# 64-feature attention two heads at a time, with GpSimd scaling the exponentials

## The reference, cut to what matters

```python
# layer 0, 8 heads: softmax over a band of 128 tokens, with a sink ("ea", bias table evb)
s = einsum('qd,kd->qk', q, k) * 64**-0.5 + bias          # masked outside the band
p = exp(s - max(s)); p = p / (sum(p) + exp(sink - max))   # o = p @ v
# layer 0, 8 heads: stick breaking ("eb"), strictly causal
a = exp(log_sigmoid(z) + log_after)                       # log_after: reverse cumulative sum of log_sigmoid(-z)
# layer 1, 16 heads: causal softmax, three dilated patterns merged in one bias table per head ("oc", odb)
# sparse block, 16 heads: causal softmax over chosen keys, one mask for all heads ("sx", s_sel)
```

## Time and profile before

| | |
|---|---|
| median of 3 runs (3391.88 to 3395.95) | 3394.07 us |
| the profiled execution's own time | 3395.51 us |
| its span, first to last instruction | 3393.7 us |
| mean granted TensorE clock | 0.975 of full speed |
| PE busy | 3284.9 us, 97% of the span |
| DVE, ACT, POOL busy | 1454.8, 1157.3, 220.9 us |
| chain that ended last | PE 90%, DVE 5%, ACT 3%, POOL 1% |

### The profile page before, as it was taken

The page is one execution under the profiler, slowest core; times in us unless marked ns, Lnnn a source line. Parts: engine busy times, 40 slices in busy tenths (PEclk is TensorE's granted clock), DMA queues, the critical chain, the costliest instruction groups (busy, mean ns, idle before and its releaser), DMA issues.

```text
span 3393.7 us, 36847 instructions
## 1 busy us (share of the span) xinstructions
PE 3284.9 (97%) x14548; PEld 2627.4 (77%) x14548; DVE 1454.8 (43%) x2354; ACT 1157.3 (34%) x1887; POOL 220.9 (7%) x439
## 2 busy tenths in 40 slices
PE   8999998999999999999999999999999999989998
PEld 6888775777788888887866877888887785768887
DVE  3332337554333243323555543332325766543332
ACT  3232334343322133223344533332226624332221
POOL 1000100010000000000400100000132100010000
PEclk9999998999999999999999999999989999989999
DMA  4322220231332323332312412333222230223331
GB/s 140 100 94 99 87 81 1 87 124 50 93 100 94 99 89 96 96 100 87 99 59 66 138 50 86 95 93 100 73 87 75 73 109 5 75 71 97 100 100 68
DMA packets 212605, 291.44 MB, mean 86 GB/s; under 512 B 13872, under 2 KB 135984, under 8 KB 212304
## 3 DMA queue, kind: packets, MB, share of 16 engines
q1 hardware_dynamic: 209792, 279.59, 26.3%
q0 software_dynamic: 2640, 9.50, 0.9%
HBM read 286.94 MB, written 2.10 MB: 85 GB/s over the span
## 4 chain that ended last, share of the span: by engine, by line
PE 90%; DVE 5%; ACT 3%; POOL 1%; issue 1%; DMA 0%; POOLq 0%; DVEq 0%; ACTq 0%
PE ps L94 87%; PE ps L97 3%; DVE ebQ L115 1%; DVE hTl L109 0%; ACT xn L100 0%; POOL stat L103 0%; DVE ebP L103 0%; ACT L100 0%; DVE ebPT L121 0%; DVE s_ri L115 0%; POOL s_ri L103 0%; DVE xn L106 0%; ACT wh L100 0%; POOL e_ss L103 0%; ACT hTh L100 0%
## 5 line engine op out<-in xcount | busy, mean ns | idle before, releaser
L103 DVE TENSOR_TENSOR wl<-raw,wh 128x1024 fp32r<-128x1024 f32 (+1 forms) x530 | 640.9, 1216 | 1249.5 <-ACT wh L100 1244.4
L100 ACT ACTIVATE wh<-raw 128x1024 fp32r<-128x1024 f32 (+1 forms) x530 | 552.4, 1051 | 1362.0 <-PE ps L94 1318.2
L94 PE MATMUL ps<-hTh,wh 128*128 128x512 f32 x2144 | 841.1, 392 | 16.6 <-DVE hTl L109 16.6
L94 PE MATMUL ps<-hTl,wh 128*128 128x512 f32 x2144 | 838.1, 391 | 0.0
L94 PE MATMUL ps<-hTh,wl 128*128 128x512 f32 x2144 | 837.6, 391 | 0.0
L94 PEld LDWEIGHTS ps<-hTh,wh 128*128 128x128 f32 x2144 | 404.9, 189 | 104.4 <-DVE hTl L109 13.7
L94 PEld LDWEIGHTS ps<-hTl,wh 128*128 128x128 f32 x2144 | 405.1, 189 | 84.7 <-issue 1.0
L94 PEld LDWEIGHTS ps<-hTh,wl 128*128 128x128 f32 x2144 | 404.9, 189 | 84.8
L94 PE MATMUL ps<-wh,hTh 128*128 128x512 f32 (+2 forms) x832 | 324.2, 390 | 10.0 <-DVE hTl L109 5.8
L94 PE MATMUL ps<-wl,hTh 128*128 128x512 f32 (+2 forms) x832 | 321.4, 386 | 0.0
L94 PE MATMUL ps<-wh,hTl 128*128 128x512 f32 (+2 forms) x832 | 321.4, 386 | 0.0
(11 more groups left out here) (347 smaller groups left out, 4076.1 us busy)
## 6 DMA issues: line engine op xcount, KB each, us to landing
raw<-in_ffn_w_gu SPq DMA_DIRECT2D x352, 256.0 KB, 3.1
raw<-in_ffn_w_down SPq DMA_DIRECT2D x88, 512.0 KB, 3.5
raw<-in_xa_w_kv SPq DMA_DIRECT2D x32, 512.0 KB, 4.0
raw<-in_w_in SPq DMA_DIRECT2D x32, 512.0 KB, 3.7
raw<-in_od_w_in SPq DMA_DIRECT2D x24, 512.0 KB, 3.6
raw<-in_w_ffn_gate SPq DMA_DIRECT2D x44, 256.0 KB, 2.9
raw<-in_w_ffn_up SPq DMA_DIRECT2D x44, 256.0 KB, 3.1
raw<-in_w_ffn_down SPq DMA_DIRECT2D x22, 512.0 KB, 3.8
```

Source lines behind the costliest of these rows:

```text
L94: return self.made(lambda e: e.matmul(*a, **k))
L100: return self.made(lambda e: e.activation(*a, **k))
L103: return self.made(lambda e: e.tensor_tensor(*a, **k))
```

## The change

`Heads` becomes `Pairs` for the four 64-feature stages: a step s now handles heads 2s and 2s + 1 (u = 0, 1).

- PE issues the score products of the two heads in turn, block by block, and the value products likewise. The blocks go in the order 3, then 2 and 0, then 1 (in the band: 2 and 3, then 1 and 0). Four banks hold scores (two groups of a pair of heads), three banks turned rows, one bank the outputs.
- The blocks' scaling by the reciprocal moves from DVE to POOL (`pool_pairs`). One reciprocal (128x8) serves both heads. It stands on DVE behind `first` of the following pair.
- ACT copies all turned groups of the even head, DVE all those of the odd head. In the stick-breaking stage ACT copies both.
- The turned rows have one buffer for each head of the pair (before: two buffers, taken in turn by successive heads).
- POOL fills four `ebQ` buffers instead of two.
- In "oc" POOL issues the bias tables of pair s + 1 behind the scaling of pair s − 1.

```diff
-            self.sgroups = [[0, 1], [2], [3]] if self.causal else [[0, 1], [2, 3]]
-            self.groups = [[3], [2, 0], [1]] if self.causal else [[0, 1], [2, 3]]
-            self.tbank = 6 - len(self.groups)
+CAUSAL_GROUPS = [[3], [2, 0], [1]]
+BAND_GROUPS = [[2, 3], [1, 0]]
+        def sbank(self, s, n, u):
+            return 2 * ((s * len(self.groups) + n) % 2) + u
+        def tbank(self, s, u, n):
+            return 4 + ((2 * s + u) * len(self.groups) + n) % 3
...
+    def pe_pairs(pe, A, qT, kT, qkey, kkey, kv_of, V, vkeys):
+        def scores(s):
...
+                for both in zip(*parts):
+                    for u, (i, W, dst) in enumerate(both):
+                        k0, k1, _, _ = A.spans[i]
+                        r = slice(64 * u, 64 * u + 64)
+                        ins = pe.matmul(dst, qT[r, s, i * P:(i + 1) * P], kT[r, kb, k0 * P:k1 * P], start=True, stop=True)
...
+        def turn(s):
+            for u in range(2):
+                for n, group in enumerate(A.groups):
+                    b, at = A.tbank(s, u, n), 0
+                    pe.wait_ge(drained, pe.held[b])
+                    pe.held[b] = (A.tag, s, "t", n, u)
+                    for i in group:
+                        k0, k1, o, W = A.spans[i]
+                        pe.wait_ge(normed, (A.tag, s, u, i))
...
+            if A.total == CAUSAL_W:
+                for kt in range(NT):
+                    for u in range(2):
+                        ins = pe.matmul(o_[64 * u:64 * u + 64, kt * P:S], V(2 * s + u, kt), A.pt[u][:, kt, kt * P:S],
+                                        start=kt == 0, stop=kt == NT - 1)
...
+        for s in range(A.N + 2):
+            if s < A.N:
+                scores(s)
+            if s >= 2:
+                values(s - 2)
+            if 1 <= s <= A.N:
+                turn(s - 1)
+
+    def turned_out(e, A, s, u):
+        for n, group in enumerate(A.groups):
+            e.wait_ge(turned, (A.tag, s, n, u))
+            if s >= 1:
+                e.wait_ge(valued, (A.tag, s - 1))
+            put_turned(e, A.pt[u], bank[A.tbank(s, u, n)], A.spans, group, (A.tag, s, n, u)).also(
+                drained, (A.tag, s, "t", n, u))
+
+    def pool_pairs(pool, A, before=none):
+        for s in range(A.N):
+            before(s)
+            rd = A.small(s, 0, 4), A.small(s, 1, 4)
+            pool.wait_ge(step, (A.tag, s, "r"))
+            for u in range(2):
+                for group in A.groups:
+                    for i in group:
+                        pool.tensor_scalar(A.row(s, u, i), A.row(s, u, i), rd[u][:, i:i + 1], None, ALU.mult).then_inc(
+                            normed, (A.tag, s, u, i))
+
+    def act_pairs(act, A, O, base_, gone):
...
+        for s in range(A.N + 2):
+            if s < A.N:
+                (sigmoids if A.stick else exps)(s)
+            if s >= 2:
+                act.wait_ge(valued, (A.tag, s - 2))
+                act_hi(act, bank[VBANK][:, :], O, base_ + s - 2, slice(0, S), gone)
+            if 1 <= s <= A.N:
+                turned_out(act, A, s - 1, 0)
+                if A.stick:
+                    turned_out(act, A, s - 1, 1)
+
+    def dve_pairs(dve, A, O, base_, bias=None):
...
+        for s in range(A.N + 2):
+            if s < A.N:
+                (before if A.stick else first)(s)
+            if 1 <= s <= A.N:
+                (breaks if A.stick else later)(s - 1)
+            if s >= 2:
+                dve.wait_ge(valued, (A.tag, s - 2))
+                dve_lo(dve, bank[VBANK][:, :], O, base_ + s - 2, slice(0, S)).also(drained, (A.tag, "o", s - 2))
+            if 1 <= s <= A.N and not A.stick:
+                turned_out(dve, A, s - 1, 1)
...
     def pool_even(pool):
+        pool_pairs(pool, EA)
         handover(pool, "stick")
         pool.memset(EB.zr[:, :], 0.0).then_inc(step, "eb zero")
         for b in range(2):
-            pool.memset(EB.q[b][:, :], 1.0).then_inc(ones_set, "eb")
+            for u in range(2):
+                pool.memset(EB.q[b][u][:, :], 1.0).then_inc(ones_set, "eb")
```

More of the change, by code:

```diff
@@ L724, in scores @@
[L724 to L748, removed]
-            if s < A.H:
[L750 to L761, removed]
-            if 1 <= s <= A.H:
[L763 to L778, removed]
-                for n, group in enumerate(A.groups):
[L780 to L793, removed]
-                value(pe, h, A.pt[h % 2])
-        attend(pe, A, own)
@@ L838, in put_turned @@
             e.wait_ge(valued, (A.tag, h - 2))
-        for i in A.groups[n]:
-            k0, k1, o, W = A.spans[i]
-            src = bank[A.tbank + n][:, at:at + W].rearrange("p (k q) -> p k q", k=k1 - k0)
-            dst = A.pt[h % 2][:, k0:k1, i * P:(i + 1) * P]
-            if e.name == "act":
-                ins = e.activation(dst, src, AF.Copy)
-            else:
-                ins = e.tensor_copy(dst, src)
-            at += W
-        ins.then_inc(put, (A.tag, h, n)).also(drained, (A.tag, h, "t", n))
@@ new lines, in act_whole @@
+    def act_whole(act, A, finish):
+        for s in range(A.H + 3):
+            if s >= 3:
+                finish(s - 3)
+            if s < A.H:
+                nm, den = A.small(s, 1), A.small(s, 2)
+                act.wait_ge(maxed, (A.tag, s))
+                if s >= 2:
+                    act.wait_ge(turned, (A.tag, s - 2, 1))
+                for i in range(NT):
+                    ins = act.activation(A.row(s, i), A.score(s, i), AF.Exp, bias=nm[:, i:i + 1], scale=A.scale,
+                                         accum_out=den[:, i:i + 1])
+                    if i % 2:
+                        ins.then_inc(drained, (A.tag, s, "s", i // 2)).also(expd, (A.tag, s))
+            if 1 <= s <= A.H:
+                whole_turned(act, A, s - 1, 0)
@@ L1523, in pe_cross, with score @@
         A = C.A
-        def score(pe, h, i, dst, k0, k1):
+        def score(pe, h, i, dst):
             for c in range(2):
@@ L1544, in value @@
                 ins.then_inc(valued, (A.tag, h, c)).also(valued, (A.tag, h))
-        pe_attend(pe, A, score, value)
+        pe_whole(pe, A, score, value)
     def act_cross(act, C):
```

415 lines of the change are left out of this document (232 added, 183 removed).

## The result

The changed kernel takes 3446.61 us (median of 4 runs, 3442.7 to 3447.81) against 3392.98 (3391.11 to 3395.95) for the kernel before in the same comparison: a ratio of 1.0156, 95% interval 1.0144 to 1.0169. It is 53.6 us slower. The profiled execution took 3447.54 us, its span is 3445.8, its mean granted clock 0.956.

The account below looks back on a forecast made before the run. PE carried 90% of the chain; paired products would leave a nearly serial loop through ACT bounding oc and sx. Savings of 1.7 (oc), 2.7 (sx), 3 (eb) and 2.3 (ea), together 9.7 us, gave 3384.5 us, range 3366 to 3406.

Parts of the forecast that it names:

- the price of POOL's scaling: Scaling of one head's blocks on POOL: 1.8 us at its copy's price, at most 3.3 at its two-input operation's price.
- POOL is beside this loop: In oc and sx, POOL's scalings from F + 3.7 finish before needed: even head by F + 5.5, odd by F + 7.3.
- these 334 us: The four changed stages ea, eb, oc and sx, together 333.9 of the 3393.7 us span; the rest should cost the same.
- PE's work per pair: Two heads on PE at 2.4 GHz: scores 2.35, values 2.3, squares 2 × 1.24, about 7.1 us instead of 11.78.
- ACT's loop: In oc and sx, PE turns the odd head only after ACT's exponentials, `hTh` and first copy: 11.5 us a pair, high clock.
- F: The start of DVE's first reduction of pair s, from which the steps of the loop in oc and sx are timed.
- My middle of 12.5 a pair: Period assumed for oc and sx, between 11.5 us at the high clock and F + 13.5 after a clock fall.
- rival 2: Loop at the low clock throughout, with longer handovers: 13.5 us a pair plus 0.3, +10, 3404 us; chance 0.23.
- Rival 3: POOL at its two-input price: scalings end near F + 10.3, tables land late, oc +9, sx hardly touched, 3394 us; chance 0.1.
- My last sign of being wrong: The prediction is wrong if, among other signs, POOL or the tables are waited for.
- The clock: PE's holes in each pair should bring the granted clock of oc and sx down to 0.7 or 0.8.
- eb and ea: Stage lengths: eb 76 us against 79.2, with 16.7 a pair at the low clock; ea 42.5 against 44.8.

Follow-up runs that it names:

- e5: Changed kernel with DVE scaling and ACT taking `hTh` and the previous pair's copies ahead of this pair's exponentials: 3328.5 us, ratio to before 0.981.
- e1: Changed kernel with the scaling by the reciprocals given back from POOL to DVE, right behind the reciprocal: 3400.3 us, ratio to before 1.0022.
- e7: Changed kernel with POOL multiplying by the constant 1.0 in place of each row's reciprocal, all waits kept: 3430.8 us.
- e4: Changed kernel with the bias tables of oc issued one pair earlier, ahead of POOL's scalings: 3442.8 us.
- e6: Changed kernel with POOL still scaling and only ACT's order altered: `hTh` and the previous pair's copies, then the exponentials: 3448.0 us.
- e8: As e5, but POOL scales one of the pair's eight blocks, the odd head's 128x512, and DVE the other seven: 3335.3 us, ratio to before 0.9829.
- e3: Changed kernel with the two heads' score products within a group, and their value products, issued in sequence instead of in turn: 3444.3 us.
- e11: As e5, but the two heads' score and value products are issued one head after the other: 3351.5 us, ratio to before 0.9876.

## Why the prediction was wrong

I predicted 3384.5 us, range 3366 to 3406, and gave "slower" 0.24. The step that failed is the price of POOL's scaling. I took 1.8 us a head and at most 3.3; it is 4.3. With it fell the statement "POOL is beside this loop": POOL's scaling is the longest part of the loop.

- **The stages.** "All of the difference must come from these 334 us" held: 51.0 of 52.1.
- **PE's work per pair.** Forecast "about 7.1 us": 7.8 measured in e5. The values paired in columns take 2.37 us, one head's time, as taken; the Trainium skill's rule that I cited for it (TensorE: Matmul & The Clock Gate, Part 3) is borne out. The scores take 2.7 for 2.35, the squares 2.77 for 2.48.
- **ACT's loop.** It was forecast rightly, but it doesn't bound the measured kernel. The first copy was to be done at F + 9.1; with F = 1804.06 it is done at F + 8.9. By my sum the odd head's squares start at once and their first four end at F + 9.8. They start at F + 9.76, because POOL holds them; that the two figures are near each other is chance. e1 shows this loop alone: with F = 1795.29 the copy is done at F + 9.2, the ten squares take 2.40 us (forecast 2.4 at the low clock), and with ACT's order changed (e5) 71.8 us go. My middle of 12.5 a pair was low by some 0.8 on average and by 1.2 in the later pairs of oc (13.66); that is rival 2 ("At 13.5 a pair", 3404), and e1 took 3400.3. So without POOL's price the forecast would have been 16 us too low, still within the range.
- **POOL: the step that failed.** "I take the copy's price, since a scaling also reads one wide operand": the number of wide operands doesn't give the price, as e7 shows, where even a constant scalar leaves 1.48 of 1.56 us. The upper bound was too low as well: I read the two-input row as 2.5 ns a column, which is the slope measured here, but without a fixed part, and a head has four instructions of about 0.28 us fixed each (0.599 us less 128 × 2.5 ns). By my own sum the odd head is then ready at F + 3.7 + 8.5 = F + 12.2, not F + 7.3; it was (1816.38 is F + 12.3), and two squares, the handovers and the first scores at the low clock (2.25 us) give the 15.3 us between two first reductions. e1, with no edit but that DVE scales in POOL's place, took 44.5 us of the 51.0 out of the four stages; in oc some 3 us of that may be the tables (e4), which POOL then issues earlier.
- **Rival 3** had "sx is hardly touched" and 3394. That was wrong even at its own price, by which the odd head is ready at F + 10.3 against F + 9.1 for the bank: it let POOL act through the tables alone. In the measured kernel the last squares, and behind them the next scores, wait for POOL itself, in sx as in oc (20.1 us longer). The tables, which I had made its sign, are 3.0 us (e4). My last sign of being wrong, "if POOL or the tables are waited for", did come true in both parts.
- **The clock** was to fall to 0.7 or 0.8 in oc and sx: 0.75 and 0.73. It rose again to 0.95 as soon as the waits went (e5), so by these runs it follows from the loops. It makes them longer in turn: the odd head's ten squares took 2.40 us in e1, the even head's 1.31. How much of e1's 13.66 is the clock no run separates.
- **eb and ea.** eb was 78.6 for 76, 0.6 under before. The length of a pair was right: the mask additions of pairs 2 and 3 start at 31.7 and 48.4 us from the stage's start (forecast 30.3 and 47.0), 16.7 apart as summed. So 1.4 of the missing 2.6 us lie before pair 2, the rest behind pair 3. ea is 43.2 for 42.5 in e1, once POOL is out of it.

## What to carry to other kernels

Before work moves to another engine, price one instruction of the same kind there, its fixed part too, times their number, and lay the sum into the loop that goes around once an iteration: what stands in the loop costs its whole length, however idle its engine was before. Where an instruction waits for two engines, compare the ends of both with its start: the profile named ACT's copy in front of the odd head's squares, and POOL's block had ended 0.7 us later. When two loops share their engines, the longer one hides the other completely (e6 against after: 0; e5 against e1: 72 us), so a fix that shows nothing may be right and only early. In an in-order queue put what frees another engine's buffer (copies out of PSUM) ahead of long work that nobody is waiting for yet (the next exponentials): with that order, DVE's scaling and the paired products, the same change is 1.9% faster than the kernel before.

## What the runs showed of the hardware that I had not expected

- GpSimd's scaling of fp32 rows costs about 0.28 us and 2.5 ns a column (0.60, 0.92, 1.24, 1.56 us for 128 to 512 columns), where its copy of 256 columns takes 0.40 and DVE's scaling of 512 takes 0.48. Its per-partition operand is 0.08 us of that (e7).
- When GpSimd and DVE scale at once, GpSimd's 128x512 takes 1.2 times as long (1560 to 1850 ns). Of DVE's four beside it two are held up by some 0.4 us each (128x384: 415 to 849 ns, 128x256: 349 to 695) and two not at all (e8).
- Value products in different column halves run beside each other fully (16 in 2.37 us) if they are issued in turn, and still partly if eight of one head follow eight of the other: 3.93 us, not twice 2.30 (e3, e11). Why they still do in part no run shows.
